# Attention units of a hybrid decoder: queries and keys turned in the middle of a unit's products and one unit on, norm steps and weight rounding in other units

## The reference, cut to what matters

```python
qa = partial_rope(rmsnorm(qa.reshape(B, T, H_A, HEAD_DIM), q_norm), pos)
ka = partial_rope(rmsnorm(ka.reshape(B, T, H_A, HEAD_DIM), k_norm), pos)
o_a = combine_by_denominators([dilated_band_stats(qa, ka, va, w, d) for (w, d) in DILATED_PATTERNS])
```

## Time and profile before

| | us |
|---|---|
| median of three runs | 3680.07 |
| profiled execution, its time | 3673.24 |
| its span | 3671.4 |
| mean granted TensorE clock in it | 0.934 |
| PE busy | 3358.6 (91%) |
| DVE busy | 2168.9 (59%) |
| ACT busy | 883.5 (24%) |
| POOL busy | 600.5 (16%) |

### The profile page before, as it was taken

One profiled execution on the slowest core, in us unless ns is written; L12 is line 12 of the kernel. 1 busy time (PEld: TensorE's weight loads), 2 busy tenths in 40 slices (PEclk: granted clock), 3 DMA queues, 4 the chain that ended last, 5 costly groups with the idle time before them and its releaser, 6 DMA issues. The chain is left out here.

```text
span 3671.4 us, 49568 instructions
## 1 busy us (share of the span) xinstructions
PE 3358.6 (91%) x19817; PEld 3084.5 (84%) x19817; DVE 2168.9 (59%) x4644; ACT 883.5 (24%) x1661; POOL 600.5 (16%) x498
## 2 busy tenths in 40 slices
PE   4888999988999999999978889997799999999989
PEld 4777767677899999998977777675798999999989
DVE  5566446657655555557566664566566555555573
ACT  4233223212311111113232323223032111111131
POOL 2001102110221221221110011111003221221211
PEclk7999989958999999999989999898599999999999
DMA  4111112343111111110211111134311111111101
GB/s 139 39 36 41 38 38 74 81 137 79 58 47 47 47 48 45 57 48 18 83 50 32 45 40 41 37 95 114 121 49 50 35 58 47 35 58 47 38 29 62
DMA packets 208269, 209.69 MB, mean 57 GB/s; under 512 B 34596, under 2 KB 180964, under 8 KB 205936
## 3 DMA queue, kind: packets, MB, share of 16 engines
q1 hardware_dynamic: 208040, 206.53, 18.7%
HBM read 175.03 MB, written 31.64 MB: 56 GB/s over the span
## 5 line engine op out<-in xcount | busy, mean ns | idle before, releaser
L763 POOL TENSOR_TENSOR wlo<-raw,whi 128x512 fp32r<-128x512 f32 (+3 forms) x488 | 599.8, 1264 | 3013.3 <-ACT whi L1251 3013.3
L779 PE MATMUL ps<-hi,wlo 128*128 128x344 f32 x2880 | 931.6, 323 | 25.7 <-DVE wb L2071 15.5
L780 PE MATMUL ps<-lo,whi 128*128 128x344 f32 x2880 | 925.0, 321 | 0.0
L781 PE MATMUL ps<-hi,whi 128*128 128x344 f32 x2880 | 924.6, 321 | 0.0
L779 PEld LDWEIGHTS ps<-hi,wlo 128*128 128x128 f32 x2880 | 546.2, 190 | 29.0 <-DVE wb L2071 16.1
L780 PEld LDWEIGHTS ps<-lo,whi 128*128 128x128 f32 x2880 | 545.5, 189 | 0.6
L781 PEld LDWEIGHTS ps<-hi,whi 128*128 128x128 f32 x2880 | 545.7, 189 | 0.0
L779 PE MATMUL ps<-whi,lo 128*128 128x512 f32 (+5 forms) x1152 | 463.0, 402 | 43.9 <-POOL wlo L763 25.6
L780 PE MATMUL ps<-wlo,hi 128*128 128x512 f32 (+5 forms) x1152 | 441.5, 383 | 0.0
L781 PE MATMUL ps<-whi,hi 128*128 128x512 f32 (+5 forms) x1152 | 441.3, 383 | 0.0
L2083 DVE TENSOR_TENSOR X<-X,ps 128x344 f32<-128x344 f32 x528 | 268.4, 512 | 196.1 <-PE ps L781 195.5
(11 more groups left out here) (273 smaller groups left out, 4333.9 us busy)
## 6 DMA issues: line engine op xcount, KB each, us to landing
raw<-in_w_up SPq DMA_DIRECT2D x44, 1024.0 KB, 5.0
raw<-in_w_in SPq DMA_DIRECT2D x112, 256.0 KB, 4.4
raw<-in_w_down SPq DMA_DIRECT2D x22, 1024.0 KB, 4.7
kvb<-in_cache_win_k SPq DMA_DIRECT2D x48, 256.0 KB, 3.1
cache<-in_cache_win_v SPq DMA_DIRECT2D x36, 256.0 KB, 5.7
x_scratch<-X SPq DMA_DIRECT2D x8, 1032.0 KB, 6.9
X<-x_scratch SPq DMA_DIRECT2D x4, 2064.0 KB, 15.0
raw<-in_w_out SPq DMA_DIRECT2D x8, 1024.0 KB, 6.5
```

The costliest lines, as they stand in the source:

```text
L763: pool.tensor_tensor(out=wlo[:, s, r], in0=raw[:, s, r], in1=whi[:, s, r].bitcast(F32), op=ALU.subtract).then_inc(w_split, 1)
L779: nc.tensor.matmul(out, a_lo, b_hi, start=first, stop=False)
L780: nc.tensor.matmul(out, a_hi, b_lo, start=False, stop=False)
L781: return nc.tensor.matmul(out, a_hi, b_hi, start=False, stop=last)
```

## The change

Four things move, and no operation is added or taken away.

- A unit's products are cut in two halves, and the turning, with its wait for `o_read`, stands between the halves instead of ahead of both.
- `norm_part`: for pairs 1 and 2 the first third of the next pair is normed in units 3, 4, 5 (before: 6, 7, 8) and the second in 8, 9, 10 (before: 9, 10, 11). Pair 0 keeps its units.
- `turn_part`: in pairs 1 and 2 the first third of the next pair is turned in units 7 and 8 (before: 9 and 10), the second stays in 12 and 13; the pair's own last third is turned in units 4 and 5 (before: 3 and 4) for pairs 1 to 3. Pair 0 keeps its units. So in pairs 1 to 3 there is one unit between the last norm step and the turning; before, and still in pair 0, the turning is in the very next unit.
- ACT rounds the weight blocks in units 3 and 5 (before: 6 and 10) of all four pairs, and the squares of the outputs move from unit 5 to unit 7.

```diff
@@ norm_part
-    if 6 <= u < 12 and p + 1 < PAIRS:
-        return (p + 1, u // 3 - 2, u % 3)
+    if p + 1 < PAIRS:
+        for x, a in enumerate((6, 9) if p == 0 else (3, 8)):
+            if a <= u < a + 3:
+                return (p + 1, x, u - a)
     return None
@@ turn_part
-    if p and u in (3, 4):
-        return (p, 2, u - 3)
-    if p + 1 < PAIRS and u in (9, 10, 12, 13):
-        return (p + 1, u // 3 - 3, u % 3)
+    if p and u in (4, 5):
+        return (p, 2, u - 4)
+    if p + 1 < PAIRS:
+        for x, a in enumerate((9, 12) if p == 0 else (7, 12)):
+            if u in (a, a + 1):
+                return (p + 1, x, u - a)
     return None
@@ tensor
                         part = turn_part(p, u)
+                        half = (ahead(u) + ahead(u + 1)) // 2
+                        products(p + 1, ahead(u), half)
                         if part:
                             pe.wait_ge(*at(o_read, NU * p + u - 1))
                             turn_third(*part)
-                        products(p + 1, ahead(u), ahead(u + 1))
+                        products(p + 1, half, ahead(u + 1))
                         turn_p(p, u)
@@ scalar
-                        if u in (6, 10):
-                            round_block(B + 2 * (p + 2) + u // 10)
+                        if u in (3, 5):
+                            round_block(B + 2 * (p + 2) + u // 5)
@@ vector
-                        if p and u == 5:
+                        if p and u == 7:
                             y_squares(p - 1, rowr[:, :], slice(4, NT))
```

## The result

The changed kernel takes 3625.4 us (median of 4 runs, 3619.8 to 3630.1) against 3680.3 us: ratio 0.9847, 95% interval 0.9835 to 0.9858, 55 us less. The forecast was 3642. The profiled execution took 3619.8 us, span 3618.0 (before 3673.2 and 3671.4).

What follows compares the result with a forecast made beforehand. PE was taken to be bound by waits, mostly for the DVE's rotation, and by the half clock behind them. Idle time 29.4 us plus clock 8 made 37.4 us, giving 3642 us; 8-in-10 range 3612 to 3662.

Steps and rivals of the forecast that it cites:

- The unnamed wait: PE's wait at the first turnings, 25.3 us in 11 waits, taken to be for `qk_norm`, whose rotation ends the DVE's unit.
- Pair 0: Half the products, 1.05 us, fill turning waits; gains in units 3, 9, 12, loss in 6; net 4.0 us a layer.
- Pairs 1 and 2: The unit between rotation and turning removes waits of 10.4 and 10.8 us; after new costs, net 4.5 and 3.9.
- Unit 4: Pairs 1 and 2: values wait for ACT's copy of queries behind root and rounding, 2.5 and 2.9 us.
- Unit 7: Pairs 1 and 2: scores wait for the mask behind a rotation that meets the second split, 1.9 and 2.2 us.
- Unit 8: Pairs 1 and 2: the keys' copy stands behind the squares of the outputs, 0.65 us.
- The idle term: PE's idle time removed over all four pairs: 14.7 us a layer, 29.4 in all.
- The clock term: 49 us at half clock cost 16 us; half given back for new waits, so 8 us gained.
- A: Rotation escapes the split, so units 6 and 7 lose less and the clock comes back whole; 3622 us, chance 0.2.
- B: Ten new waits in two layers each bring a half-clock stretch, so the clock gain vanishes; 3655 us, chance 0.18.
- C: Slower: recurring waits in units 4 to 8 keep pairs 1 and 2 at half clock; up to 3749 us, chance 0.04.
- D: Nothing moves: the DVE's chain refills PE's gaps in each unit; 3680 us, chance 0.06.

Runs made afterwards that it cites:

- shift_only: Kernel before with only norm steps, turnings and the outputs' squares moved to the new units, products and rounding as before; 3626.5 us.
- mid_only: Kernel before with only the turning put between the halves of the unit's products; 3638.7 us.
- copy_first: Changed kernel with a pair's first rounding moved from unit 3 to unit 4, right behind the copy of the turned queries; 3619.5 us.
- old_round: Changed kernel with the rounding back in units 6 and 10; 3609.9 us.
- the change's second profile: Profile of the changed kernel run once more with no edit; 3626.1 us.
- pieces8: Changed kernel with every split in 8 pieces instead of 4; 3610.1 us.
- best: Changed kernel with roundings moved in pairs 0 to 2, pair 0's turnings in 7, 8, 10, 11, 13, 14, and outputs' squares in unit 6; 3588.1 us.
- free_round: Changed kernel with roundings in units 12 and 13 of pair 0, 6 and 11 of pairs 1 and 2, 3 and 5 of pair 3; 3600.8 us.
- mid_round: Kernel before with the turning between the halves of the products and rounding in units 3 and 5, norm steps unmoved; 3614.7 us.

## Why the prediction was right, step by step

- **The unnamed wait is the rotation.** Shown: with a unit between them (shift_only) it is gone in pairs 1 to 3, and half the products ahead (mid_only) take 1.0 to 1.3 us off nine of the eleven waits (unit 9 of pair 2 had 0.4 us to lose, pair 3 lost 1.6).
- **Pair 0.** Turnings after, predicted and measured: unit 3 1.1 and 0.93; unit 6 3.7 and 3.0; unit 9 0.55 and 0.46; unit 12 less than 2 and 1.8. Units 4 and 10 gain nothing, as said: 4.3 and 5.4 us long before and after.
- **Pairs 1 and 2.** Unit 4: 2.5 and 2.9 predicted, 2.25 and 2.68 measured, and copy_first and old_round show that the rounding is all of it but 0.9. Unit 7: 1.9 and 2.2 predicted, 1.8 and 3.5 measured; in pair 2 the split held three steps of the rotation, not two. Unit 8: 0.65, measured 0.5 and 0.7. The sum of the waits in the earlier trace rows, "about 21" predicted, is 20.2 with the new ones.
- **What was mis-sized.** The idle term: 29.4 us predicted, 35.8 measured. Most of it is the 0.1 us charged for each of 22 turnings a layer, 4.4 us in two layers: unit 13 of pair 1 has the same work with its turning in the middle, and takes 6.71 us against 6.76. The clock term: 8 predicted, 14.0 measured. The half that I took back for the new waits was nearly right, some 20 of 49 us at half clock are left. Its price was not: 2.8 / 11 = 0.255 us for a matmul is a mean over transposes of 128 columns and matmuls of 384, with matmuls that only reach into the window counted whole. Rows of one sort, starts at half clock and then at full clock behind the same turning of the kernel before:

```profile
292.35 0.52 PE L779 MATMUL ps<-whi,lo 128*8 128x384 f32 x1
292.67 0.52 PE L780 MATMUL ps<-wlo,hi 128*8 128x384 f32 x1
...
294.12 0.34 PE L779 MATMUL ps<-whi,lo 128*8 128x384 f32 x1
294.29 0.33 PE L780 MATMUL ps<-wlo,hi 128*8 128x384 f32 x1
```

They are 0.32 us apart and then 0.17, so a us at half clock costs 0.46 to 0.47 us and not 0.32. The 49 us cost some 23, not 16, and the fall from 49 to 20 makes 13 of the 14.0 measured. The prices of rivals A and C are too low by the same factor. Idle time and clock together are 49.8 instead of 37.4, the whole miss but for 3.6 us outside the units; both terms erred to the same side. Inside the idle term unit 7 of pair 2 cost 1.3 us a layer more than charged, and smaller errors the other way cover that.
- **Rivals.** A (the rotation escapes the split) fell: two or three of its steps are held, 0.93 us and more each. Its 3622 is nearer to the measured time than the forecast, but that is luck: it came of idle time and clock that were worth more, not of the rotation. B fell: the clock gave more than forecast, though three of its five new waits a layer (four in the change's second profile) were followed by half clock. C fell: the mean clock rose from 0.97 and 0.96 to 0.98. D fell: PE's idle time fell by 35.8 us.
- **What the prediction did not see**: that the shift alone would give the whole gain, and that the rounding's move, right for the kernel before, costs 17 us once norm steps stand in units 3 to 5 (11 without the middle). Each cost was in the prediction, under pairs 1 and 2; that they outweigh what the move gives elsewhere was not worked out, because the sum was made against the kernel before and not against the change without this part.

The Trainium skill, page "SBUF — State Buffer", section "Who interferes with whom", says of the ports that VectorE and GpSimd share that whoever issues first has them for the whole instruction. pieces8 agrees: the hold follows the piece, 0.53 us at 0.56 and 0.93 at 0.97.

## What to carry to other kernels

When a change has parts, sum it once against the kernel before and once for each part against the change without it: a part can be a gain alone and a loss among the others. In engines that run in order, look at what stands in front of a short copy that another engine waits for; a rounding of 1.5 or 1.9 us with no hurry of its own cost 1.4 us in pair 1 and 1.8 in pair 2 that way, and moving it a few lines took that away. Price half clock from rows of one sort of matmul, at either level, and not from a count over a mixed window. Put a spare unit between producer and consumer before filling the wait with work.

## What the runs showed that I had not expected

- A wait costs more than its length through the clock. PE's busy time in the two layers' units is 608.1 us before, 594.1 after, 584.0 in best, for the same matmuls.
- The granted clock falls behind waits of 1.4 us (free_round, unit 8 of pair 2) to 3.5 us but not behind all of them: of two profiles of the changed kernel the one has half clock in pair 2 at unit 7, the other at unit 5. In one execution of mid_round the first layer has half clock behind unit 6's 3.0 us in pair 0, and the second has none.
- Cutting POOL's splits finer, at more POOL time in all, made the program 13 to 16 us faster; 10.6 to 12.8 us of it lie in the units, where PE waits for what the DVE does behind the hold.
